# Adding the shared expert's rows to the rank sums on GpSimd instead of VectorE

## The reference

```python
def _swiglu(x, wg, wu, wd):
    return (jax.nn.silu(x @ wg) * (x @ wu)) @ wd

def _moe(h, ...):
    ...
    _, idx = lax.top_k(jnp.where(emask, sel, -jnp.inf), TOP_K)      # TOP_K = 8 of 64 experts
    w = jnp.take_along_axis(scores, idx, axis=-1)
    w = w / jnp.sum(w, axis=-1, keepdims=True) * ROUTED_SCALE
    routed = _routed_experts(xf, idx, w, w_exp_gate, w_exp_up, w_exp_down)
    shared = _swiglu(xf, w_sh_gate, w_sh_up, w_sh_down)
    return (routed + shared).reshape(b, t, d)

def _layer(x, ...):
    ...
    f = _moe(h, w_router, router_bias, w_exp_gate, w_exp_up, w_exp_down,
             w_sh_gate, w_sh_up, w_sh_down)
    x = x + g2 * _rms_norm(f, norm_post_ffn)
    return x, s_ret_new, s_gla_new
```

## Time and profile before

| | |
|---|---|
| median of 3 runs | 1336.88 us (1336.25 to 1337.11) |
| the profiled execution | 1338.04 us, span 1335.8 us |
| PE busy | 1207.8 us (90%) |
| DVE busy | 887.0 us (66%) |
| ACT busy | 601.3 us (45%) |
| POOL busy | 163.4 us (12%) |
| transfers | 339.20 MB, mean 254 GB/s |

### The profile page before, as it was taken

How to read it: one execution, slowest core, us unless ns; L and a number is a source line. 1 busy time by engine, 2 the same in 40 slices (tenths; PEclk the granted TensorE clock), 3 DMA queues, 4 the chain that set the end, 5 groups by cost and what they waited for, 6 DMA issues and landing times.

```text
span 1335.8 us, 18616 instructions
## 1 busy us (share of the span) xinstructions
PE 1207.8 (90%) x5990; PEld 828.7 (62%) x5990; DVE 887.0 (66%) x1362; ACT 601.3 (45%) x712; POOL 163.4 (12%) x184
## 2 busy tenths in 40 slices
PE   5899999896899999999999999999999999999810
PEld 0799999754334244444777777777777777777500
DVE  0711442245465357575788888888888888888888
ACT  1422222203221012222677767767767767767501
POOL 0100000000011001101112212212212211221002
PEclk7799999986899999999999999999999999999955
DMA  9332221505135631537999999999999999999896
GB/s 372 138 112 74 74 74 37 130 0 189 63 126 170 230 129 39 142 119 264 355 380 395 389 383 385 378 376 382 375 369 374 377 378 381 374 379 359 348 318 221
DMA packets 91519, 339.20 MB, mean 254 GB/s; under 512 B 12312, under 2 KB 35880, under 8 KB 65420
## 3 DMA queue, kind: packets, MB, share of 16 engines
q1 hardware_dynamic: 75104, 301.02, 61.5%
q0 software_dynamic: 16384, 37.78, 8.1%
HBM read 317.24 MB, written 42.48 MB: 269 GB/s over the span
## 4 chain that ended last, share of the span: by engine, by line
PE 81%; DMA 8%; DVE 7%; ACT 2%; SPq 1%; issue 1%; DVEq 0%; POOLq 0%; POOL 0%; ACTq 0%
PE ps L1650 14%; PE ps L2033 13%; PE ps L2017 8%; PE ps L2013 7%; PE ps L2015 7%; PE ps L2014 7%; PE ps L1999 4%; PE ps L1863 4%; PE ps L1681 3%; DMA arena<-in_w_ada 3%; DMA arena<-expert_rows 2%; PE ps L1891 2%; PE ps L1912 1%; PE ps L1990 1%; PE ps L2023 1%
## 5 line engine op out<-in xcount | busy, mean ns | idle before, releaser
L1493 DVE TENSOR_TENSOR gu_lo<-w_gu,gu_hi 128x1536 fp32r<-128x1536 f32 x128 | 224.4, 1754 | 0.9 <-ACT gu_hi L1011 0.9
L1011 ACT ACTIVATE gu_hi<-w_gu 128x1536 fp32r<-128x1536 f32 x128 | 189.9, 1483 | 0.0
L1488 DVE TENSOR_TENSOR down_lo<-arena,down_hi 128x2048 fp32r<-128x2048 f32 x64 | 146.7, 2293 | 38.5 <-ACT down_hi L1017 38.5
L2013 PE MATMUL ps<-gu_hi,xT_hi 128*112 128x512 f32 x384 | 156.8, 408 | 0.9 <-issue 0.9
L2015 PE MATMUL ps<-gu_hi,xT_lo 128*112 128x512 f32 x384 | 151.2, 394 | 0.0
L2014 PE MATMUL ps<-gu_lo,xT_hi 128*112 128x512 f32 x384 | 150.8, 393 | 0.0
L1650 PE MATMUL ps<-w_hi,hT_hi 128*128 128x300 f32 (+1 forms) x480 | 145.0, 302 | 1.0 <-DVE w_lo L1093 1.0
L1650 PE MATMUL ps<-w_lo,hT_hi 128*128 128x300 f32 (+1 forms) x480 | 144.6, 301 | 0.0
L1650 PE MATMUL ps<-w_hi,hT_lo 128*128 128x300 f32 (+1 forms) x480 | 144.5, 301 | 0.0
L1017 ACT ACTIVATE down_hi<-arena 128x2048 fp32r<-128x2048 f32 x64 | 122.0, 1906 | 2.2 <-DMA arena<-in_w_exp_down 1.9
L2017 PE MATMUL ps<-w_gu,arena 128*112 128x512 f32 x256 | 120.2, 592 | 0.0
(11 more groups left out here) (271 smaller groups left out, 1932.1 us busy)
## 6 DMA issues: line engine op xcount, KB each, us to landing
w_gu<-in_w_exp_gate SPq DMA_DIRECT2D x64, 1024.0 KB, 10.3
w_gu<-in_w_exp_up SPq DMA_DIRECT2D x64, 1024.0 KB, 17.5
arena<-in_w_exp_down SPq DMA_DIRECT2D x64, 1024.0 KB, 12.7
arena<-in_w_ada SPq DMA_DIRECT2D x24, 1024.0 KB, 7.6
arena<-in_w_in SPq DMA_DIRECT2D x12, 1200.0 KB, 5.4
arena<-expert_rows SPq DMA_DIRECT2D x9, 1024.0 KB, 13.3
arena<-expert_rows SPq DMA_DIRECT2D x4, 2048.0 KB, 11.3
arena<-in_x_prompt SPq DMA_DIRECT2D x8, 512.0 KB, 8.7
```

The source lines that it names most:

```text
L1011: a.activation(gu_hi[b % RING][:, :, ks], w_gu[b % U][:, :, ks], ACT.Copy).then_inc(s_ghi, 1)
L1488: v.tensor_tensor(down_lo[:, :, :], w_dn[b % RING], down_hi[:, :, :].bitcast(F32), ALU.subtract).then_inc(s_dlo, 1)
L1493: v.tensor_tensor(gu_lo[b % U][:, :, ks], w_gu[b % U][:, :, ks], gu_hi[b % RING][:, :, ks].bitcast(F32), ALU.subtract).then_inc(s_glo, 1)
L2013: pe.matmul(out, x_hi, gu_hi[r][:, :, k], start=(k == 0), stop=False)
```

## The change

POOL, when it has seen the last scatter land and raised `s_tick` to 1, waits for the shared rows and adds them to `ffn_sum[t]`, tile by tile in LAST_ORDER; each add raises `s_tick` by one, to 2 to 6. DVE's `middle_ranks` no longer adds the shared rows; it adds the two middle ranks to each other and then waits for `s_tick` of its tile before it adds them to `ffn_sum[t]`. DVE's wait for `s_bcg` ahead of the first middle tile stays, and so do SP's waits.

```diff
--- before.py
+++ after.py
@@ -475,7 +475,7 @@
         s_y = sem("y_psum")
         s_ya = sem("y_rows_ready")
         s_ys = [sem(f"y_rows_out{b}") for b in range(U)]
-        s_tick = sem("rows_scattered")
+        s_tick = sem("rows_scattered_then_shared_added")
         s_free = sem("y_rows_free")
         s_wt = sem("slot_weight_and_row_ready")
         s_pulse = sem("gpsimd_pulse")
@@ -791,6 +791,11 @@
             turn(last, True)
             g.wait_ge(s_ys[U - 1], 16 * last + 16)
             g.sem_inc(s_tick, 1)
+            g.wait_ge(s_bcg, 16 * (1 + SB + 2))
+            for n, t in enumerate(LAST_ORDER):
+                R = ROWS[t]
+                g.wait_ge(s_add, t + 1)
+                g.tensor_tensor(ffn_sum[t][0:R], ffn_sum[t][0:R], shared[0:R, t], ALU.add).then_inc(s_tick, 1)
             for n, t in enumerate(LAST_ORDER):
                 R = ROWS[t]
                 g.wait_ge(s_q3, n + 1)
@@ -1551,9 +1556,9 @@

             def middle_ranks(t, done):
                 R, y, to = ROWS[t], ranks_mid[t][0:ROWS[t]], ffn_sum[t][0:ROWS[t]]
-                step(v.tensor_tensor(to, to, shared[0:R, t], ALU.add))
                 v.wait_ge(s_yb[t], 32)
                 step(v.tensor_tensor(y[:, 0], y[:, 0], y[:, 1], ALU.add))
+                v.wait_ge(s_tick, 1 + (done - NT))
                 mark(v.tensor_tensor(to, to, y[:, 0], ALU.add), s_add, done)

             def high_ranks(n, t):
```

## The result

The changed kernel took 1340.57 us in the median of 16 runs, the kernel before 1335.32 us in 16 runs beside it: a ratio of 1.0041 with a 95% interval of 1.0023 to 1.0059. Timed again, in 12 runs against 35, it was 1339.22 us against 1336.65 us, 1.0020 (0.9999 to 1.0040). (The ratios are those on record; they differ a little from the quotient of the two medians, which is 1.0039 for the first timing.) The first timing shows the changed kernel slower, and the second has 1 only just inside its interval. The amount is small beside what two executions of one kernel differ by: the 35 runs reach from 1330.9 to 1343.4 us.

A forecast was written before the change was run, and what follows sets the result against it. Bound at its end by a DVE chain, rank rows just ahead: middle ranks 4.2 us later, less 0.68 us of waiting, net +3.5 us on a median of 1336.88, giving 1340.4 us (+0.26%); 8-in-10 range 1336.4 to 1342.8.

The forecast's parts named there:

- the sum in which someone is always at work: Middle ranks, from 1285.5: POOL and DVE take turns without idling, 24.3 us in all, ending at 1309.8, 4.2 us later.
- The rival without a collision: Middle ranks: DVE is not held by POOL; gain 0 to 1.8 us, taken as 0.7, giving 1336.2 us; chance 0.15.
- the partial rival: Middle ranks: POOL holds the port only for its reads, 1.8 us, or its add is nearer 1.8; 1337.9 us; chance 0.13.
- POOL's add: Each of five POOL adds of shared rows, 1024 columns: taken as 2.3 us, between bounds of 0.9 and 2.7.
- the 0.62: Chance given to the forecast itself, exclusion with POOL adds of 2.1 to 2.5 us, 1339.4 to 1341.4 us.
- the third high load: High-rank rows of the third tile: issued at about 1305, landing at 1312.6 to 1315, needed only at 1318.0.
- the 0.68 us of waiting: DVE's wait for the third tile's high-rank rows, which was to go away and reduce the 4.2 us.
- The 25.9 us that I gave for the rest of the work: From the high ranks to the store: work and root waits, claimed to stay 25.9 us.
- The start of POOL: POOL's first add of shared rows: begins at 1285.5, 2.5 us before the first middle rows.
- the best case is capped by x1 and the third load: End of the kernel without a collision: x1 and the high loads, not DVE, limit the gain to 0 to 1.8 us.

The follow-up runs named there:

- no_shared: The kernel before without the adds of the shared rows on any engine (their load stays); one run, 1334.21 us beside 1340.34 us for the kernel before.
- one_column: The changed kernel, but GpSimd adds only the first of 1024 columns of the shared rows; 1336.03 us against 1336.65 before, ratio 0.9989.
- two_first: The kernel before, but VectorE adds the first two tiles' shared rows ahead of its wait for middle rows; 1335.76 us against 1336.65, ratio 0.9996.

## Why the prediction was right, and what was off in it

The direction and the mechanism held. The two engines exclude each other, DVE is held by POOL as POOL was by DVE, and the sum in which someone is always at work is what the trace shows: 5 adds and 10 instructions fill 1287.84 to 1310.62 without a hole. The rival without a collision is refuted by every DVE instruction of 3.24 us. Of the partial rival one half is refuted for an add of two inputs, that POOL holds DVE for less than its add takes (2.00 us by itself, 2.01 us of holding). Its other half, an add nearer to 1.8 us, is partly what came.

The step that was off is a size, POOL's add: I took 2.3 us, between bounds of 0.9 and 2.7, and it is 2.00, outside the 2.1 to 2.5 us for which I gave the 0.62. The sum gave 24.3 us for this stretch, the trace has 22.8: 5 x 0.3 = 1.5 us. So the middle ranks end 2.5 us later against the last low-rank sum (26.19 us behind it and 23.65 us), and not 4.2.

A second size was off as well, the third high load. I had it land at 1312.6 to 1315, 3 us or more before it is needed, from a sum of x1, the second and the third load (4.5 MB rather than the 4.3 I wrote). It was asked for at 1305.60 and 1305.38, near the 1305 that I had, but in the second profile of the changed kernel DVE waits for it:

```profile
1319.17 1.23 DVE L1567 TENSOR_TENSOR arena<-arena 128x1024 f32<-128x1024 f32 x1 [0.64 <-DMA arena<-expert_rows]
```

That is 13.8 us behind its issue, and not 7.6 to 10. The fourth and fifth loads, asked for 2.5 and 5.0 us behind it, were not in my sum; whether they are what slowed it is not shown. So the 0.68 us of waiting went away in one pair of profiles and not in the other: the load was waited for 0.7 and 0.0 us before, 0.0 and 0.6 us after. With the 2.5 and 2.6 us of the middle ranks this gives the 1.9 and 3.2 us by which the stretch grew, 2.6 us on the mean, against 3.5 forecast. (The 25.9 us that I gave for the rest of the work should read 26.45, 1332.74 - 1305.61 - 0.68; nothing was worked out from it.)

That the median came out 0.2 us from the forecast is luck. I started from a median of 1336.88 us, and the 16 runs of the kernel before have 1335.32. The difference that I forecast was 3.5 us; 2.6 us are explained and shown, the first timing has 5.3 us and the second 2.6. The start of POOL was right (it waited for the shared rows, and began as they landed, 3.4 us behind the last low-rank sum and 3.5 in the forecast), as was the claim that even the best case is capped by x1 and the third load: no_shared and one_column show it, with 0 to 2 us for the removal of all five adds against my 0 to 1.8, in one profile each.

On the Trainium skill's rule (SBUF — State Buffer, "Who interferes with whom"): what it says on two-input VectorE instructions and GpSimd instructions that read is what the traces show, and that one which only writes does not contend, too. Its words that whoever issues first has the shared pair "for the whole instruction" stand there of VectorE's 2-port modes, and the prediction carried them over to two-input instructions. For the two-input add that is borne out (2.01 of 2.00 us), for the copy it is not (0.71 of 1.03 us). Half of the figure in the Trainium skill (GPSIMD Engine Reference, "Performance versus the Vector engine"), 2.25 us, is 0.25 us above what the add of 1024 columns took here.

## What to carry to other kernels

Before moving an elementwise instruction to GpSimd to relieve VectorE, look at what VectorE runs beside it: if those instructions read two operands from SBUF, the two take turns (no run here has VectorE at one operand beside such an add), and an add of 1.23 us on VectorE is exchanged for 2.00 us on the same resource; only what falls in a hole of VectorE is free, and the hole can be used by VectorE itself, as in two_first. And bound the gain first by leaving the work out: here even that brought 0 to 2 of the 5 us of the stretch, since the transfers were just behind.

## What was not expected of the hardware

A copy of 1024 float32 columns on GpSimd takes 1.03 us where it comes first, but in the turns that follow it holds a two-operand VectorE instruction for only 0.71 us. An add that reads the same tile as both inputs takes 1.89 us and holds for 1.57, against 2.00 and 2.01 with two tiles. Why the copy and the one-tile add hold for less than they take is not shown. In the five profiles with GpSimd adds or copies of 1024 columns neither engine has two instructions in a row while both have work: GpSimd's gets in at the end of each of VectorE's, in a gap of 0.03 us.
